# Expert weight loads of 2 MB, each made as two loads of 1 MB with semaphores of their own

## What is computed

```python
logits = (h @ p['router_w']).astype(jnp.float32) + p['router_b'].astype(jnp.float32)
top_logit, top_idx = lax.top_k(logits, TOP_K)      # 4 of 32 experts for each token
...
gu = xblk @ p['moe_w_gu'][e] + p['moe_b_gu'][e]    # 1024 x 2048
glu, lin = gu[:, :EXPERT_FF], gu[:, EXPERT_FF:]
...
act = glu * jax.nn.sigmoid(SWIGLU_ALPHA * glu) * (lin + 1.0)
return act @ p['moe_w_down'][e] + p['moe_b_down'][e]   # 1024 x 1024
```

## Time and profile before

| | |
|---|---|
| median of 3 runs | 1312.89 us (1307.82 to 1312.96) |
| profiled execution, its own time | 1311.34 us |
| its span in the profile | 1309.6 us |
| PE busy | 1192.1 us, 91% |
| DVE, ACT, POOL busy | 24%, 17%, 3% |
| bytes moved by DMA | 459.94 MB, 351 GB/s over the span |
| SP's queue | 41,152 packets, 451.98 MB |

### The profile page before, as it was taken

One profiled execution on the slowest core, in us unless ns is written; L12 is line 12 of the kernel. 1 busy time (PEld: TensorE's weight loads), 2 busy tenths in 40 slices (PEclk: granted clock), 3 DMA queues, 4 the chain that ended last, 5 costly groups with the idle time before them and its releaser, 6 DMA issues.

```text
span 1309.6 us, 17312 instructions
## 1 busy us (share of the span) xinstructions
PE 1192.1 (91%) x7132; PEld 482.5 (37%) x7132; DVE 313.3 (24%) x632; ACT 228.7 (17%) x381; POOL 39.4 (3%) x70
## 2 busy tenths in 40 slices
PE   4989997888999999999999999999999999999994
PEld 1335576674433333333333333333233333333231
DVE  1203667553311121111111111111112111111113
ACT  2102254532211111111111111111111111111112
POOL 0300100000000000000000000000000000000000
PEclk9989999799899999999999999999999999999998
DMA  9988000238489999999999999999999999999991
GB/s 372 356 310 322 6 2 3 73 111 361 177 344 426 431 425 431 426 426 431 425 428 429 426 430 426 428 428 425 429 428 428 429 428 428 428 427 428 428 429 63
DMA packets 44241, 459.94 MB, mean 351 GB/s; under 512 B 5112, under 2 KB 7328, under 8 KB 16432
## 3 DMA queue, kind: packets, MB, share of 16 engines
q1 hardware_dynamic: 41152, 451.98, 82.4%
q0 software_dynamic: 2576, 6.35, 1.6%
q10 hardware_dynamic: 480, 1.13, 0.2%
HBM read 457.96 MB, written 1.47 MB: 351 GB/s over the span
## 4 chain that ended last, share of the span: by engine, by line
DMA 50%; PE 42%; DVE 3%; ACT 3%; issue 1%; SPq 0%; DVEq 0%; ACTq 0%
DMA ring<-in_moe_w_gu_dram 47%; PE bank L1168 15%; PE bank L569 5%; PE bank L1188 4%; PE bank L962 2%; DMA ring<-in_w_mod_dram 2%; DMA ring<-in_w_in_dram 2%; PE bank L683 2%; PE bank L1131 1%; PE bank L1146 1%; PE bank L546 1%; PE bank L559 1%; PE bank L668 1%; PE bank L1158 1%; PE bank L929 1%
## 5 line engine op out<-in xcount | busy, mean ns | idle before, releaser
L1168 PE MATMUL bank<-ring,proj 128*64 128x512 f32 x2048 | 458.4, 598 | 32.9 <-DMA ring<-in_moe_w_gu_dram 32.9
L1168 PEld LDWEIGHTS bank<-ring,proj 128*64 128x64 f32 x2048 | 140.3, 137 | 349.5 <-issue 274.9
L1188 PE MATMUL bank<-ring,proj 128*64 128x512 f32 x1024 | 233.9, 598 | 11.9 <-DVE proj L2058 11.9
L2049 DVE TENSOR_SCALAR proj<-bank 128x512 f32<-128x512 f32 x32 | 22.1, 692 | 479.7 <-PE bank L1168 479.7
L1525 ACT ACTIVATE proj<-proj 128x512 f32<-128x512 f32 x32 | 20.2, 630 | 603.9 <-DVE proj L2049 603.9
L1188 PEld LDWEIGHTS bank<-ring,proj 128*64 128x64 f32 x1024 | 69.1, 136 | 131.8 <-issue 131.8
L569 PE MATMUL bank<-ring,hT 128*128 128x512 f32 (+2 forms) x224 | 92.7, 571 | 7.7 <-DMA ring<-in_w_in_dram 5.0
L2061 DVE COPY proj<-bank 128x512 f32<-128x512 f32 x32 | 22.1, 691 | 249.1 <-PE bank L1188 249.1
L1146 PE MATMUL bank<-proj 64*128 64x512 f32 x256 | 63.6, 615 | 0.0
L569 PEld LDWEIGHTS bank<-ring,hT 128*128 128x128 f32 x224 | 43.3, 197 | 54.4 <-issue 41.1
L1131 PE MATMUL bank<-h_nat,proj 128*64 128x512 f32 x264 | 62.3, 593 | 0.0
(11 more groups left out here) (332 smaller groups left out, 805.5 us busy)
## 6 DMA issues: line engine op xcount, KB each, us to landing
ring<-in_moe_w_gu_dram SPq DMA_DIRECT2D x128, 2048.0 KB, 24.4
ring<-in_moe_w_down_dram SPq DMA_DIRECT2D x64, 2048.0 KB, 21.7
ring<-in_w_mod_dram SPq DMA_DIRECT2D x12, 2048.0 KB, 12.8
ring<-in_w_in_dram SPq DMA_DIRECT2D x5, 2048.0 KB, 17.3
ring<-in_w_out_dram SPq DMA_DIRECT2D x2, 2048.0 KB, 8.5
const_sb<-in_constants_dram POOLq DMA_DIRECT2D x1, 2450.0 KB, 17.6
ring<-in_w_in_dram SPq DMA_DIRECT2D x1, 1536.0 KB, 8.7
ring<-in_w_in_dram SPq DMA_DIRECT2D x1, 1024.0 KB, 5.6
```

Source lines behind the costliest of these rows:

```text
L1168: mm = pe.matmul(b[CAP * half:CAP * half + CAP, :], xT[:, k % 4, k // 4, :], ring[:, j, 2048 * kc + o + 512 * half:2048 * kc + o + 512 * h ...
L1188: mm = pe.matmul(b_down[CAP * half:CAP * half + CAP, :], aT[:, k % 4, k // 4, :], ring[:, 4 + j, D * kc + 512 * half:D * kc + 512 * half + ...
L2049: ts(moe["glu"], bank[4][:, :], LIMIT, None, ALU.min).then_inc(sem("glu_sb"), 1)
```

## The change

Each expert load is two DMAs of 1 MB, one for the first 2048 floats of a partition's slot and one for the second. The second has a semaphore of its own, `ring_rest[j]`. PE waits for `ring_full[j]` before the first half of a slot's matmuls and for `ring_rest[j]` before the second half, and adds 1 to `ring_used[j]` after each half. SP waits for each half by itself: for the first until `ring_used[j]` is 2e - 1, for the second until it is 2e. DVE's two waits have doubled values. Bytes, slots, matmuls and their order stay.

```diff
+HALF = SLOT // 2
...
+        ring_rest = [sem(f"ring_rest{i}") for i in range(NSLOT)]
...
-            def expert_load(e, j):
+            def expert_load(e, j, n=0):
...
-                src = rows[:, SLOT * (j % 2):SLOT * (j % 2) + SLOT] if j < 4 else rows
-                sp.dma_start(ring[:, j, :], src).then_inc(ring_full[j], 16)
+                lo = SLOT * (j % 2) if j < 4 else 0
+                for k, landed in enumerate((ring_full[j], ring_rest[j])):
+                    if not isinstance(e, int):
+                        sp.wait_ge(ring_used[j], 2 * n + k - 1)
+                    sp.dma_start(ring[:, j, HALF * k:HALF * k + HALF], rows[:, lo + HALF * k:lo + HALF * k + HALF]).then_inc(landed, 16)
...
             with sp.Fori(1, NE) as e:
                 for j in range(NSLOT):
-                    sp.wait_ge(ring_used[j], e)
-                    expert_load(e, j)
+                    expert_load(e, j, e)
...
                 for j in range(4):
-                    pe.wait_ge(ring_full[j], 16 * (n + 1) + 16 * FRONT_ROUNDS[j])
                     for kc in range(2):
+                        if kc == 0:
+                            pe.wait_ge(ring_full[j], 16 * (n + 1) + 16 * FRONT_ROUNDS[j])
+                        else:
+                            pe.wait_ge(ring_rest[j], 16 * (n + 1))
...
-                    mm.then_inc(ring_used[j], 1)
+                        mm.then_inc(ring_used[j], 1)
...
-                    pe.wait_ge(ring_full[4 + j], 16 * (n + 1) + 16 * FRONT_ROUNDS[4 + j])
                     for kc in range(4):
+                        if kc == 0:
+                            pe.wait_ge(ring_full[4 + j], 16 * (n + 1) + 16 * FRONT_ROUNDS[4 + j])
+                        if kc == 2:
+                            pe.wait_ge(ring_rest[4 + j], 16 * (n + 1))
...
-                    mm.then_inc(ring_used[4 + j], 1)
+                        if kc % 2:
+                            mm.then_inc(ring_used[4 + j], 1)
...
-                dve.wait_ge(ring_used[3], n + 1)
+                dve.wait_ge(ring_used[3], 2 * n + 2)
...
-                dve.wait_ge(ring_used[5], n + 1)
+                dve.wait_ge(ring_used[5], 2 * n + 2)
```

More of the change, by code:

```diff
@@ L445, in _ @@
                         for j in range(NSLOT):
-                            sp.wait_ge(ring_used[j], b * NE + e)
-                            expert_load(e, j)
+                            expert_load(e, j, b * NE + e)
             sp.wait_ge(sem("y_ready"), 2)
```

## The result

The changed kernel takes 1322.5 us, the median of 5 runs (1319.9 to 1328.7), against 1310.1 us before in the same session: 12.4 us more. The ratio over all runs is 1.0102 with a 95% interval of 1.0070 to 1.0134, which is 13.4 us. A second series, against 26 runs of the kernel before, gave 1.0093 (1.0074 to 1.0111). The forecast was 9.5 us slower, 1322.4 us.

The account below looks back on a forecast made before the run. The prediction took the never-pausing DMA weight stream to bound the kernel from about the tenth expert. Its terms, -2.0 - 1.7 + 13.2 = +9.5 us, gave 1322.4 us, range 1310 to 1330 (the forecast's own 1315.5 to 1329.9).

Parts of the forecast that it names:

- What bounds the kernel: From about the tenth expert, PE is fed by a DMA stream that never pauses: 29.53 us a turn, 4.92 us a slot.
- Term 3: Expert loads in the loop: 8 KB packets and one more completion cost 72 ns a slot, +13.2 us over 184 slots.
- the prediction's formula: Per slot: two 8 KB packet times less one 16 KB packet's 615.2 ns, times 8 partitions, plus about 10 ns per completion.
- The middle of three short stretches: 311.5 ns for an 8 KB packet, chosen from w_mod's loads in SP's queue: 309.1, 311.9 and about 314 ns.
- near zero: Packet cost under the skill's rule: engines do not care for 8 or 16 KB, sum -3.7 us, 1309.2 us; chance 0.12.
- Term 2: End of the last expert: only half of slot 3's matmul work follows PE's last wait, -1.7 us.
- Term 1: Start of the loop's load stream: SP refills half a slot once PE has passed it, 363.1 instead of 365.18, -2.0 us.
- No gap: Loop's first turn: slot 4's first half is free at 382.5, while eight halves keep the engines busy to 385.1.
- paid once: The 2.3 us latency from a load's issue to its data counts only once for the whole stream.
- Term 4: SP's twelve issues a turn at 0.33 us, PE's further waits and two more loads ahead of the loop stay hidden: nothing.
- The sum: Whole kernel: -2.0 - 1.7 + 13.2 = +9.5 us, with bounds of +2.6 to +17.0 us.
- Rival D: Each of 184 further loads shows its 2.3 us of latency: +423 us, 1736 us; chance 0.01.

## Why the prediction was right, point by point

- **What bounds the kernel**: right. Every change to the packets moved the turn, and the finer hand-over, which took 6.6 us off PE's waits, did not.
- **Term 3, +13.2 us**: right in sum. Two loads alone cost 74 ns a slot and 13.3 us in the table's stretch to PE's last start on slot 3, where 72 and 13.2 were forecast. Its parts were not right. A packet costs 9.3 ns, not 7.8, and a completion about nothing, not 10. And the loop's packets took 313.9 ns, not 311.5, which by the prediction's formula gives 111 ns a slot. What that formula left out is that packets overlap: their times add up to 101.2% of the engines' time now and to 100.5% before. Divided by the share, 310.2 and 612.1 ns, it gives 2 x 310.2 - 612.1 = 8.3 ns, 66 a slot; the shares are given to 0.1%, which leaves some 5 ns of a slot open. The middle of three short stretches was luck to that extent.
- **The rule weighed there**: "DMA: Bandwidth & Descriptors" of the Trainium skill (section "Why small descriptors are slow") has an overhead per packet, but holds joining descriptors worth it only up to 256 B. That is said of putting small pieces together in one packet, while here the pieces themselves were made longer or shorter, so the forecast's "near zero" asked more of the rule than it says. In this kernel, where the DMA engines are the bound, making 16 KB packets 32 KB long took 0.13 us off a turn, and cutting them to 8 KB put 0.45 on it.
- **Term 2, -1.7 us**: right, 1.7 and 1.6 us in the two profiles.
- **Term 1, -2.0 us**: the step that failed. SP's first load did come 1.5 and 1.7 us sooner. But the stream was taken to keep its full pace from there on ("No gap", the latency "paid once"), and it did not. Against the two loads handed over whole (921.20 us) the stream of the change was 3.0 and 1.0 us longer. In the first profile slot 4 was issued 20.1 us after the first load, not 19.4, and the engines' share fell to 0.89 there; in the second there was no gap at slot 4 (shares of 1.01), and the early start was lost in slow windows at the start alone.
- **Where the 3.0 and 1.0 us lie**: the traces hold the times of the 16 completions of each load, one for each engine's part, and PE starts after the last. For the last load of the last slot 3, in us from SP's first load:

  | profile | first completion | last completion | between them |
  |---|---|---|---|
  | before | 904.3 | 907.8 | 3.5 |
  | two loads, no finer hand-over | 918.1 (estimate) | 921.2 | 3.1 |
  | the change | 919.4 | 924.1 | 4.8 |
  | the change, second profile | 918.7 | 922.2 | 3.5 |

  (The estimate: that slot's two loads share a semaphore there; its first completion of all is at 915.6, and a half takes 2.48 us.) So of the 3.0 us some 1.3 are a later stream and 1.7 are engines further apart; of the 1.0 us it is 0.6 and 0.4. The later stream is there after the first turn: 12 MB after its start the change is 1.4 and 0.6 us behind the two loads handed over whole. The engines also part in the dips: over the six slots of expert 1 the time between the first and last completion of a load grows from 0.5 to 2.2 us in the first profile and from 0.5 to 1.9 in the second, and only from 0.4 to 0.7 before. The rest grows slowly over the loop in each of the four profiles. Why some engines lose more than others was not found.
- **Term 4, nothing**: right in sum. DVE starts with the norm gains at 314.03 in the second profile (314.14 before) and has PE's output at 329.09 (329.14 before), so the two further loads ahead of the loop are hidden. But SP's issue did not stay at 0.33 us, as the last section shows; it was covered all the same.
- **The sum**: forecast +9.5; 13.1 and 10.9 us by the table, 12.4 and 12.2 us by the medians. What is missing is in the main term 1, given back. That the time itself came within 0.1 us (1322.4 against 1322.5) is luck: the forecast was added to a median of three runs, 1312.89 us, and the kernel before has 1310.1 us over five and 1311.2 over 26.
- **Rival D**, the fixed time of a load showing: it did not, as the share of 101.2% and the turns say. The Trainium skill's "SBUF — State Buffer" (section "The DMA setup-cost knee") gives every transfer about 2 us; the load alone in the queue shows such a latency, 2.3 us, but with ten loads outstanding a further load cost 74 ns, all of it the packets'.

## What to carry to other kernels

When a queue of loads is the bound, ask first what the edit does to the engines' time per byte, and only then what it does to waits: PE's longest wait halved here and the kernel got slower. Split a load where its wait ends the chain (the last one), not in each turn, and merge loads in the middle, leaving a few turns of the finer kind before the end so that the consumer can catch up. Don't count an earlier start of a stream as won before its first turn is looked at: here it went into a gap or into slower first loads each time. Effects of a few microseconds are read from a late, steady period and from an anchor behind the part that scatters, not from the span.

## What was not expected of the hardware

- What the queue holds is not a number of bytes. A load of 1 MB in the change lands a median of 25.0 us after its issue, some ten loads of 2.49 us, and SP is held in the issue itself. Line 384 from 400 to 1250 us (min, median, max in ns):

```profile
L384 SPq DMA_DIRECT2D ring<-in_moe_w_gu_dram x230: 332/1344/3986, 400.1 to 1234.8; - x115
...
DMA to landing us min/median/max: 9.4/25.0/27.9
```

  With loads of 512 KB the median to landing is 15.0 us, some twelve of 1.29 us, and their issues take a median of 0.94 us. So about 10 MB are outstanding in the one and 6 MB in the other when SP is held. Both kinds have 128 packets a load, and no run tells whether the limit is in loads or in packets. Smaller loads thus also shorten what the queue covers. It cost nothing here; handed over whole, the loads of 1 MB are issued in a median of 0.33 us, 1.79 at most.
- Where a stream starts with single halves, the packets themselves are slower: 370 GB/s at a share of 1.02, where the loop has 421. That the nearly empty queue is the reason is not shown. The first two full windows of 2.5 us had 406 and 419 GB/s in the kernel before, with one or two loads of 2 MB outstanding, and 429 and 423 in the version with two loads of 1 MB issued together.
- The 16 engines drift apart in a long stream: the completions of one load lie 0.4 us apart at the start of the loop in the kernel before and 3.5 us at its end, and PE waits for the last.
- The packet's price is nearly the same over the whole range tried: 9.3 ns from 16 to 4 KB, about 8 from 32 to 16 KB.
